# Six modulation chunks of layer 1: row sums on VectorE in place of a matmul on TensorE

## What is computed

```python
mod = silu(c) @ w_ada[l] + b_ada[l]                 # 1024 x 6144: shift, scale, gate, twice
sh1, sc1, gt1, sh2, sc2, gt2 = split(mod, 6)
h = modulate(rms_norm(x, g_mix[l]), sh1, sc1)       # h * (1 + scale) + shift
z = h @ w_in[l]                                     # conv, neighbourhood and window attention, gates
x = x + gt1 * ((sum of sigmoid(gate_i) * (branch_i @ w_branch[i])) @ w_out)
x = x + gt2 * expert_choice_ffn(modulate(rms_norm(x, g_ffn[l]), sh2, sc2))   # 16 experts, 12 MB each
```

## Time and profile before

| | us |
|---|---|
| median of three runs | 1844.44 (1844.4 to 1846.84) |
| span of the profiled execution | 1846.3 |
| TensorE busy (matmuls) | 1689.6 (92%) |
| VectorE busy | 771.0 (42%) |
| ScalarE busy | 478.0 (26%) |
| chain that ended last: TensorE, DMA, VectorE | 68%, 23%, 4% |

### The profile page before, as it was taken

One profiled execution on the slowest core, in us unless ns is written; L12 is line 12 of the kernel. 1 busy time (PEld: TensorE's weight loads), 2 busy tenths in 40 slices (PEclk: granted clock), 3 DMA queues, 4 the chain that ended last, 5 costly groups with the idle time before them and its releaser, 6 DMA issues.

```text
span 1846.3 us, 26514 instructions
## 1 busy us (share of the span) xinstructions
PE 1689.6 (92%) x10854; PEld 977.2 (53%) x10854; DVE 771.0 (42%) x1746; ACT 478.0 (26%) x1052; POOL 111.4 (6%) x149
## 2 busy tenths in 40 slices
PE   5999999999998999999898799989999997777866
PEld 2887777777674333333232398877883332222222
DVE  3455556674434233333323665577753222111111
ACT  3324455552223100000000434465441000000001
POOL 1001210000001000000000101300001000000000
PEclk8999999999998999999999999999998999999998
DMA  9532322127778999999999764337899999999996
GB/s 353 154 91 69 106 72 80 35 81 256 251 286 326 409 428 427 428 428 428 427 429 426 271 206 133 96 115 252 282 364 385 426 426 426 426 425 426 426 426 281
DMA packets 152035, 543.83 MB, mean 295 GB/s; under 512 B 10026, under 2 KB 92400, under 8 KB 126700
## 3 DMA queue, kind: packets, MB, share of 16 engines
q1 hardware_dynamic: 149104, 535.35, 74.0%
q0 software_dynamic: 2400, 6.16, 1.2%
q10 hardware_dynamic: 412, 0.64, 0.1%
HBM read 539.13 MB, written 2.98 MB: 294 GB/s over the span
## 4 chain that ended last, share of the span: by engine, by line
PE 68%; DMA 23%; DVE 4%; ACT 2%; SPq 2%; issue 1%; POOL 0%; DVEq 0%; ACTq 0%
PE bank L2158 20%; PE bank L2019 12%; PE bank L2020 11%; PE bank L2021 11%; DMA ring<-in_w_exp_down 8%; DMA ring<-in_w_exp_gate 7%; DMA ring<-in_w_exp_up 4%; DMA spare<-in_w_exp_gate 3%; PE bank L2132 2%; PE bank L2048 2%; PE bank L2071 2%; PE bank L1934 2%; PE bank L2058 2%; PE bank L2187 1%; DMA ring<-in_w_ada 1%
## 5 line engine op out<-in xcount | busy, mean ns | idle before, releaser
L2158 PE MATMUL bank<-ring,XEP 128*32 128x256 f32 (+1 forms) x2384 | 384.9, 617 | 37.1 <-DMA ring<-in_w_exp_gate 20.7
L2019 PE MATMUL bank<-HH,WH 128*128 128x512 f32 (+1 forms) x864 | 312.1, 361 | 5.7 <-DVE HL L1627 4.7
L2020 PE MATMUL bank<-HL,WH 128*128 128x512 f32 (+1 forms) x864 | 300.4, 348 | 0.0
L2021 PE MATMUL bank<-HH,WL 128*128 128x512 f32 (+1 forms) x864 | 299.9, 347 | 0.0
L2158 PEld LDWEIGHTS bank<-ring,XEP 128*32 128x32 f32 (+1 forms) x2384 | 114.1, 130 | 277.5 <-issue 227.8
L1598 DVE TENSOR_TENSOR WL<-ring,WH 128x1024 fp32r<-128x1024 f32 (+1 forms) x172 | 185.0, 1078 | 133.4 <-ACT WH L1362 132.6
L1856 DVE TENSOR_TENSOR X<-X,bank 128x512 f32<-128x512 f32 x184 | 114.0, 682 | 188.2 <-PE bank L2187 100.0
L2019 PEld LDWEIGHTS bank<-HH,WH 128*128 128x128 f32 x864 | 163.8, 190 | 54.0 <-issue 25.9
L1362 ACT CAST WH<-ring 128x1024 fp32r<-128x1024 f32 (+1 forms) x172 | 158.0, 926 | 100.5 <-PE bank L2021 64.7
L2158 PE MATMUL bank<-ring,HIDT 128*32 128x256 f32 (+1 forms) x1232 | 153.6, 481 | 31.3 <-DMA ring<-in_w_exp_down 31.3
L2021 PEld LDWEIGHTS bank<-HH,WL 128*128 128x128 f32 x864 | 163.8, 190 | 21.2
(11 more groups left out here) (244 smaller groups left out, 1955.4 us busy)
## 6 DMA issues: line engine op xcount, KB each, us to landing
ring<-in_w_exp_gate SPq DMA_DIRECT2D x55, 2048.0 KB, 30.9
ring<-in_w_exp_up SPq DMA_DIRECT2D x49, 2048.0 KB, 34.4
ring<-in_w_exp_down SPq DMA_DIRECT2D x48, 2048.0 KB, 36.6
ring<-in_w_ada SPq DMA_DIRECT2D x48, 1024.0 KB, 7.4
ring<-in_w_in SPq DMA_DIRECT2D x40, 1024.0 KB, 6.3
split_slot<-in_w_exp_up SPq DMA_DIRECT2D x8, 2048.0 KB, 29.3
split_slot<-in_w_exp_down SPq DMA_DIRECT2D x8, 2048.0 KB, 33.5
ring<-in_w_in SPq DMA_DIRECT2D x28, 512.0 KB, 5.2
```

The source lines that it names most:

```text
L2019: mm(t, wh, hi[:, k, 0:b.n], start=k == 0, stop=False)
L2020: mm(t, wh, lo[:, k, 0:b.n], start=False, stop=False)
L2021: last = mm(t, wl, hi[:, k, 0:b.n], start=False, stop=k == b.kk - 1)
L2158: last = mm(out_bank[tw * g:tw * g + tw, 0:nw], stationary(k), w[:, g::G] if spread else w[:, nw * g:nw * g + nw], start=k == 0, stop=k == ...
```

## The change

The six `ada` calls of layer 1 for chunks 4 to 9 go. In their place ScalarE's queue loads a chunk's rows (two halves of 1 MB) to `row_place`, which lies over `spare`. VectorE multiplies each of the eight row blocks (128 partitions x 512) by its CS value and sums them in ROWSUM, one `form` step at a time; TensorE sums over the partitions and turns in one, with four matmuls that have ROWSUM as weights and a column of ones (twice) as the moving side, and does that twice for SC2. VectorE's finish is then a copy instead of a reduction. Behind the first two ac blocks the loads of chunk 4 go out; its first form comes 28 k-steps later, then one every third k-step; four k-steps behind the last form the next chunk's loads go out, and `ada2` follows the next block's end. The first expert load (place 9) waits for `formed` and moves behind the window attention. Nothing changes in layer 0.

```diff
@@ plan @@
+ROW_AFTER, ROW_EVERY, ROW_LAG = 28, 3, 4
@@ finish_block @@
         P.add("done", blk=b)
+        if P.rows_last is not None and P.ticks - P.rows_last[0] >= ROW_LAG:
+            P.deferred.append(P.rows_last[1])
+            P.rows_last = None
@@ emit @@
         if kind == "k":
             P.add("k", blk=atom[1], k=atom[2])
             turn_due(1)
+            form_due()
@@ make_plan @@
+    def rows(l, c):
+        n = P.formed
+        P.formed += 2
+        P.add("row_load", l=l, col=c, n=n // 2, before=n)
+        s = Step(kind="ada2", layer=P.layer, l=l, v=c // 2, half=c % 2, formed=P.formed)
+        def turn():
+            s.out = [P.tile(dve=True) for _ in range(2 if s.v == SC2 else 1)]
+            P.mods += len(s.out)
+            P.steps[P.layer].append(s)
+        P.rows_due = [Step(kind="form", layer=P.layer, l=l, k=k, n=n // 2, formed=n + 1 + k // 4, out_tile=turn) for k in range(KD)]
+        P.rows_from = P.ticks + ROW_AFTER
+
+    def form_due():
+        P.ticks += 1
+        if P.rows_due and P.ticks >= P.rows_from and (P.ticks - P.rows_from) % ROW_EVERY == 0:
+            s = P.rows_due.pop(0)
+            P.steps[P.layer].append(s)
+            if not P.rows_due:
+                P.rows_last = P.ticks, s.out_tile
+                P.rows_from = P.ticks + ROW_LAG
+        elif not P.rows_due and P.rows_left and P.ticks >= P.rows_from:
+            rows(P.layer, P.rows_left.pop(0))
@@ layer 1, behind the first two ac blocks @@
                     run([("done", head), ("done", b)])
+                    P.rows_left = [5, 6, 7, 8, 9]
+                    rows(l, 4)
@@ behind the convolution @@
-        if last:
-            expert_load(Step(o_ready=("ht_ready", 2 * KD)))
@@ window attention @@
-            if last:
-                mid = len(sums) // 2
-                now = ((4,), (5, 6), (7,), (8,))[p]
-                sums = sums[:mid] + [("call", ada(l, now[0]))] + sums[mid:] + [("call", ada(l, c)) for c in now[1:]]
             attention("sw", p, info, atoms + sums)
             info = nxt
         o_sw = P.obs
+        if last:
+            expert_load(Step(o_ready=("formed", P.formed)))
@@ branch sums @@
-        if last:
-            mods[9] = mod_load(9)
-            following = dpair(2, 1)
-        else:
+        if not last:
...
-            now = 9 if last else 4 + 2 * d2
+            now = 4 + 2 * d2
@@ buffers @@
+        row_place = [sb(f"row_place{i}", [128, 4, 512], at_) for i, at_ in enumerate((R_X + 8192, R_MRG + 8192))]
+        ROWSUM = sb("ROWSUM", [128, 512], R_PT + 8192)
@@ scalar @@
+                    elif kind == "row_load":
+                        act.wait_ge(ht_ready, KD * DEPTH)
+                        for r in range(2):
+                            if s.before:
+                                act.wait_ge(formed, s.before - 1 + r)
+                            act.dma_start(row_place[r][:], source(("w_ada", s.l, 512 * s.col, 512, 4 * r, 4))).then_inc(rows_in[r], 16)
@@ vector @@
-                reduced(nc.vector.tensor_reduce(sums, turned, AX.X, ALU.add))
+                if s.formed:
+                    reduced(nc.vector.tensor_copy(sums, turned))
+                else:
+                    reduced(nc.vector.tensor_reduce(sums, turned, AX.X, ALU.add))
...
+                    elif kind == "form":
+                        w = row_place[s.k // 4][:, s.k % 4, :]
+                        if s.k % 4 == 0:
+                            dve.wait_ge(rows_in[s.k // 4], 16 * (s.n + 1))
+                        cs = CS[:, s.k, 0:1]
+                        if s.k == 0:
+                            ins = nc.vector.tensor_scalar(ROWSUM[:], w, cs, None, ALU.mult)
+                        else:
+                            ins = nc.vector.scalar_tensor_tensor(ROWSUM[:], w, cs, ROWSUM[:], ALU.mult, ALU.add)
+                        if s.k % 4 == 3:
+                            ins.then_inc(formed, 1)
+                            dve.wait_ge(formed, s.formed)
+                        else:
+                            link(ins)
+                    elif kind == "ada2" and s.formed:
+                        for i, t in enumerate(s.out):
...
+                            dve.wait_ge(blk_ready, t.ready)
+                            finish_modulation(s, BLK[t.bank][:, 0:8].rearrange("p (k s) -> p k s", s=2), (RED, REDN)[i], copied, natural=i == 1)
@@ tensor @@
+                    elif kind == "ada2" and s.formed:
+                        pe.wait_ge(formed, s.formed)
+                        for i, out_ in enumerate(s.out):
+                            t = open_tile(out_)
+                            for k in range(4):
+                                cols = slice(k, 512, 4) if i == 0 and s.v in (SH2, SC2) else slice(128 * k, 128 * k + 128)
+                                last = mm(t[:, 2 * k:2 * k + 2], ROWSUM[:, cols], SLOTS[:, 0:1].broadcast_to((128, 2)), start=True, stop=True)
+                            last.then_inc(blk_ready, 1)
```

More of the change, by code:

```diff
@@ L102, in __init__ @@
                  dve=None, end=None, expert=None, first=None, gate=None, grp=None, gt_free=None, half=None, hh=None, hts=None,
-                 i=None, info=None, k=None, kind=None, kk=None, l=None, layer=None, lg=None, lt=None, lts=None, early=None, turned=None, mods=None, n=None, normalised=None,
+                 i=None, info=None, k=None, kind=None, kk=None, l=None, layer=None, lg=None, lt=None, lts=None, early=None, formed=None, turned=None, mods=None, n=None, normalised=None,
                  nk=None, ns=None, ntt=None, o_ready=None, o_ready_need=None, ord=None, out=None, out_tile=None, p=None, pair=None,
@@ L147, in __init__ @@
         self.early = early
+        self.formed = formed
         self.turned = turned
@@ L217, in __init__ @@
         self.rope_due = []
+        self.rows_due, self.rows_left, self.rows_last = [], [], None
+        self.ticks = self.formed = self.rows_from = 0
     def add(self, kind, **kw):
@@ L665, in make_plan @@
                 mods[c] = mod_load(c, *homes[c % 2])
-            following = dpair(2, 1)
+        following = dpair(2, 1)
         for d2 in range(4):
@@ L700, in make_plan @@
                     mods[7 + 2 * d2] = mod_load(7 + 2 * d2, SLOT * 3, Step(used_tile=P.tiles))
+        assert not P.rows_due and not P.rows_left and P.rows_last is None
         P.c_tile = P.tiles
@@ L1001, in hybrid_dit_kernel @@
         gt2_in = sem("gt2_in")
+        formed = sem("formed")
+        rows_in = [sem(f"rows_in{r}") for r in range(2)]
         sq_ready = sem("sq_ready")
@@ L1063, in hybrid_dit_kernel @@
         zeroed = sem("zeroed")
-        sem_named = {"dve_evicted": dve_evicted, "qk_ready": qk_ready, "mrg_ready": mrg_ready, "ht_ready": ht_ready, "pv_ready": pv_ready}
+        sem_named = {"dve_evicted": dve_evicted, "qk_ready": qk_ready, "mrg_ready": mrg_ready, "ht_ready": ht_ready, "pv_ready": pv_ready, "formed": formed}
         w_in = [sem(f"w_in{j}") for j in range(NWIN)]
```

3 lines of the change are left out of this document (added).

## The result

The changed kernel takes 1861.2 us (median; 1858.0 to 1864.5) where the kernel before, on the same chip, takes 1844.4 (1843.7 to 1846.8). The ratio is 1.0085, 95% interval 1.0069 to 1.0100: 0.85% or 15.7 us slower. Forecast were 6.3 us, and the range ended at 1856.5: the direction is right, the size is too small by more than half.

A forecast was written before the change was run, and what follows sets the result against it. Bound: the expert-weight stream, its start set by layer 1's dense part. Costs of 17.7 us (1.7 + 4.0 + 5.2 + 5.0 + 1.8) less 11.4 returned gave 6.3 us slower, 1850.7 us; range 1840.5 to 1856.5.

The forecast's parts named there:

- what bounds the kernel, and how the tail answers: Tail is one expert-weight stream started by layer 1's dense part; each us at the branch sums' end moves the end one.
- The return of 11.4 us: From 1250 us on, sections and the stretch behind them get shorter without their modulations and turns: 11.4 us in sum.
- TensorE's own balance: TensorE gives up 15.1 us (`ada` calls, transposes) and gains 6.9 us of narrow matmuls: 8.2 us less work.
- VectorE's queue in order: In attention, forms before a wait eat that wait; the rest delays the second normalise or the next section's first maximum.
- the 5.2 of chunk 7: Section of 1164.51: 1.1 us from forms ahead, TensorE standing 3.9 us for the last form; 5.2 us longer in all.
- Rival 3: More than the sum: TensorE standing near 1175 and 1245 loses its clock, +3.4 to 6.8 us, 1854 to 1857.5; chance 0.12.
- the cover of chunks 4 and 5: Convolution and V: VectorE's idle time covers the first two chunks' forms; each costs only 0.86 us on TensorE, +1.7 us.
- VectorE over 0.9 busy in the long sections: Sign: in the sections of chunks 6, 7, 8, longer by 4 to 5 us, VectorE would be over 0.9 busy.
- the two signs: Chunks 6 to 8: either a TensorE wait for `formed`, or waits for PB grown from 4.6 us to over 8.
- Rivals 1 and 2: 1: waits swallow the forms, at best 1836.2, chance 0.16. 2: chunks 6 and 9 covered, 1845.7, no change, chance 0.22.
- rival 4: Row place freed too late, loads wait for `formed` on ScalarE and casts queue behind them; given nothing of its own.
- The moved expert load: First expert load, 2 MB, goes from 1060.71 to about 1290: cost nothing, or 4.9 us if it slid into the full stream.

The follow-up runs named there:

- e2_no_sums: Changed kernel without VectorE's forms and the row loads; TensorE's turning matmuls stay but read a constant: 1838.2 us, ratio 0.9958.
- e15_sums_alone: The kernel without forms and row loads, with the 48 forms put back reading a constant, still no row loads: 1850.8 us, ratio 1.0027.
- The staircase: Runs adding one part at a time, against before: TensorE's side -7.7 us, forms +5.0, row loads +6.7, TensorE's waits for the sums +15.7.
- e4_filled: Changed kernel with 36 idle matmuls run by TensorE while it waits for chunk 7's sum: 1857.2 us, ratio 1.0063.
- e5_three_early: Changed kernel summing only chunks 4 to 6, all ahead of attention, a form every second step; 7 to 9 through TensorE; first expert load earlier: 1858.5 us, ratio 1.0072.
- e1_unread: Changed kernel whose turning matmuls read a constant and wait for no sum; forms and row loads stay: 1852.6 us, ratio 1.0036.
- e12_load_last: Kernel with chunks 4 to 6 summed early and spread, with the first expert load put back behind the window attention: 1845.2 us, ratio 1.0001.
- e16_shifted: Kernel with chunks 4 to 6 early and expert load behind the window attention, 18 steps instead of 22 from load to first form: 1844.5 us, ratio 0.9995.
- e11_three_spread: Changed kernel summing only chunks 4 to 6, spread, chunk 6 written in reading order; 7 to 9 through TensorE; expert load earlier: 1849.0 us, ratio 1.0012.

## Why the prediction was right and wrong

**Right: what bounds the kernel, and how the tail answers.** The end followed the end of the branch sums one to one. The return of 11.4 us is 11.6 in the trace.

**Right: TensorE's own balance.** 8.2 us less work by the sum, 7.7 us less time in e2_no_sums. The group of narrow matmuls is 0.95 us for contiguous columns (0.86 from the 32-column row). For the four chunks read with a stride the row that I took was the wrong one: 2.0 us. In the total it can't be seen. As a part of the sum this side was too good: without the forms and the waits for sums it had 1.7 - 11.4, 9.7 us less, and 7.7 was measured.

**Right: VectorE's queue in order, roughly.** Forms of 796 and 479 ns (790 and 520 in the sum, their links included), 12.7 us in all when alone (e15_sums_alone against e2_no_sums). In the prediction the forms and small steps carried about 12 us: 4.0 for chunk 6, the first 1.1 for chunk 7, 4.9 for chunk 8, 1.8 for chunk 9. But this 12.7 has some half clock of its own in it, so the agreement is partly luck: the section of chunk 7 is 3.2 us longer through forms alone where I had 1.1.

**Wrong: a wait of TensorE was counted at its own length.** This is the step that failed. The staircase has 9.0 us for the waits for sums; the prediction had about 4.1, the 5.2 of chunk 7 less its 1.1 of forms. That is 4.9 of the 9.4 us that the sum lacked; the rest is the 2.0 above and what the forms and row loads took more than their 12, 0.7 and 1.7. For chunk 7 the sum had 3.9 us of standing and nothing behind it. TensorE came to the group 6.9 us into the section (6.7 forecast), but the sum only at 11.7 instead of 10.5: it stood 4.82 us, and the clock fell, 1.9 us more (e4_filled). The section's 8.0 us are 3.2 of forms, 2.9 of standing and 1.9 of clock, where I had 1.1, 4.1 and nothing: the standing itself was priced too high, the forms too low, the clock not at all. Chunk 6's turns wait 1.71 us and up to 3.3 us of lost clock follow (14.81 beside 11.51 us); behind the 3.17 us wait at 1223 the section is 1.6 us or more longer than in e2_no_sums, also in kernels without any wait for sums, in part by its own forms.

Rival 3 had the mechanism and a price of 3.4 to 6.8 us. It named two stretches, 1175 and 1245; the first is right, in place of the second there were three (1143, 1224, 1259), the first two of them behind waits for PB of 1.7 and 3.2 us. It also held it possible only for long standing, since waits of up to 1.5 us in the earlier trace rows leave the clock at 1.00. The line between the two is not where I drew it: in e5_three_early the clock fell behind one of 1.51 us.

**Wrong: the cover of chunks 4 and 5.** The groups cost what I had, 1.8 us (e2_no_sums: first scores at 83.3 us, 81.5 before). Beside them TensorE stood 1.35 us for chunk 4's sum. In the first blocks steps are 0.36 us long, and a lag of four steps is 1.4 us: I had counted cover in steps and in VectorE's mean idle time, not in the length of a step at that place. e5_three_early makes the same mistake larger, and I made it again in its forecast.

**Wrong in what would show it.** VectorE over 0.9 busy in the long sections: it is 0.65 to 0.82 in those of chunks 6 to 8 (13.28 of 18.00 for chunk 7). Of the two signs of which one was to come, the wait for the sum came (4.82 us); the waits for PB went from 4.6 to 5.7 us, not to 8. With the wait for the sum gone they are 8.2 (e1_unread): each hides a part of the other.

**Rivals.** Rivals 1 and 2 are out: no section absorbed its forms. (Rival 2's number has a slip: chunks 6 and 9 stand in the sum with 5.8 us, not 5, so it comes to 1844.9.) Of rival 4 a small part is there: loads do wait for the sums on ScalarE, 5.4 us once, and moving them gave 1.7 to 2.6 us at most. The moved expert load went out at 1264.69 and not about 1290. No run moves it alone; nothing in the trace speaks of a cost, and e12_load_last and e16_shifted have it in the same place and are level with before. In e11_three_spread, at another place, it cost two sections 5 us.

**Open.** What decides in one execution whether the clock falls behind a wait of 1.7 us, and why chunk 6's section lost clock in every profile in which TensorE read the sums. Not tried: the other order of the sums in all chunks, and the whole change with all its waits filled.

## What to carry to other kernels

Work given to an idle engine is paid at the waits that it makes for the busy one: cost such a wait at its length plus the clock behind it, and look at the granted clock of each section first when a change costs more than its sum. Cover is to be counted in microseconds at the place, not in steps of a plan whose length differs between stages. Before comparing two profiles, find the last row that the change can't touch and count from there; here this alone moved the difference from 12.1 to 15.0 us.

## What the runs showed of the hardware

- TensorE's granted clock fell to the lower of its two levels behind waits of 0.28 and 1.71 us ahead of two turns in some executions and not in others (0.77 and 0.90 in one kernel, 1.00 twice in e1_unread), and once behind 1.51 us in an attention without forms (0.87). At chunk 7's wait of 4.3 to 4.8 us it fell each time (0.81, 0.81, 0.83, 0.80), and not in the two profiles with 36 idle matmuls in it (1.00 twice); 12 idle matmuls in the wait of 1.71 us did not keep it (0.87). In all eleven profiles with a wait of 3.2 us near 1220 the section behind it has 0.73 to 0.89.
- A stationary fp32 matrix of 128x128 read with a stride of four elements doubles the time of a narrow matmul: four of them 1.91 us, contiguous 0.95.
- GpSimd's `tensor_scalar` on 128x512 fp32 takes 1926 ns with 1377 for the addition; VectorE does both at once in 796 ns.
- VectorE's `scalar_tensor_tensor` on 128x512 fp32 takes 750 ns with its columns in order and 1128 ns when it reads the rows with a stride of four.
- A 2 MB load beside the weight stream of the attention: two sections 5.0 us longer at DMA shares of 1.11 and 1.04.
